# Block-2 modulation vectors: four matmuls against a column of ones in place of four transposes and a row sum

## The reference, cut to what matters

```python
cond = jax.nn.silu(c)                       # (1, 1024)
for l in range(DEPTH):
    mod = cond @ ada_w[l] + ada_b[l]        # ada_w[l]: 1024 x 9216
    sh1, sc1, ga1, sh2, sc2, ga2, sh3, sc3, ga3 = jnp.split(mod, 9, axis=-1)
    n = _modulate(_rms_norm(h, norm_g[l, 0]), sh1, sc1)
    h = h + 0.5 * ga1 * _swiglu(n, ffn_w_in[l, 0], ffn_w_out[l, 0])
    ...
```

## Time and profile before

| | before |
|---|---|
| median of 3 runs | 2551.77 us (2551.61 to 2553.09) |
| profiled execution, its own time | 2551.77 us |
| its span (first to last instruction) | 2550.0 us |
| mean granted TensorE clock | 0.986 of full speed |
| busy share: TensorE matmul / weight load | 96% / 82% |
| busy share: VectorE / ScalarE / GpSimd | 65% / 47% / 8% |

### The profile page before, as it was taken

The page is one execution under the profiler, slowest core; times in us unless marked ns, Lnnn a source line. Parts: engine busy times, 40 slices in busy tenths (PEclk is TensorE's granted clock), DMA queues, the critical chain, the costliest instruction groups (busy, mean ns, idle before and its releaser), DMA issues.

```text
span 2550.0 us, 34014 instructions
## 1 busy us (share of the span) xinstructions
PE 2447.2 (96%) x13945; PEld 2086.7 (82%) x13945; DVE 1656.3 (65%) x2149; ACT 1202.5 (47%) x1441; POOL 215.2 (8%) x334
## 2 busy tenths in 40 slices
PE   7999999999999999899999999989999999998998
PEld 5888998788788899788788798878877879887886
DVE  4786777787776686778668665575555456557444
ACT  4445464444443546443444436944444443694443
POOL 2000002000100000300010000210000000021000
PEclk9999999999999999999999999999999999999999
DMA  8784455786887454688588554455556545445553
GB/s 291 260 298 149 148 166 190 256 297 231 274 292 235 132 158 156 221 272 297 179 275 304 184 158 133 133 180 188 200 168 206 189 152 157 136 131 184 198 182 103
DMA packets 369162, 514.25 MB, mean 202 GB/s; under 512 B 21600, under 2 KB 310614, under 8 KB 369008
## 3 DMA queue, kind: packets, MB, share of 16 engines
q1 hardware_dynamic: 342608, 415.80, 50.6%
q0 software_dynamic: 26400, 96.28, 10.7%
HBM read 510.89 MB, written 1.13 MB: 201 GB/s over the span
## 4 chain that ended last, share of the span: by engine, by line
PE 83%; DVE 8%; ACT 4%; issue 3%; POOL 1%; DMA 0%; SPq 0%; DVEq 0%; POOLq 0%; ACTq 0%
PE ps L1658 76%; DVE lo L1083 3%; ACT hi L708 2%; PE ps L1704 2%; PE ps L1680 1%; PE ps L1834 1%; PE ps L1844 1%; DVE arena L1572 1%; POOL T L641 1%; PE ps L1806 1%; DVE arena L1142 1%; PE ps L1853 1%; ACT arena L748 0%; DMA raw<-in_ffn_w_gu 0%; DVE X L1116 0%
## 5 line engine op out<-in xcount | busy, mean ns | idle before, releaser
L1083 DVE TENSOR_TENSOR lo<-raw,hi 128x2048 fp32r<-128x2048 f32 (+1 forms) x400 | 908.5, 2273 | 541.8 <-ACT hi L708 541.0
L708 ACT ACTIVATE hi<-raw 128x2048 fp32r<-128x2048 f32 (+1 forms) x400 | 757.7, 1897 | 508.4 <-PE ps L1658 494.4
L1658 PE MATMUL ps<-hi,NH 128*128 128x512 f32 (+3 forms) x1760 | 681.5, 387 | 38.1 <-DVE lo L1083 14.8
L1658 PE MATMUL ps<-hi,NL 128*128 128x512 f32 (+3 forms) x1760 | 672.3, 382 | 0.0
L1658 PE MATMUL ps<-lo,NH 128*128 128x512 f32 (+3 forms) x1760 | 671.9, 382 | 0.0
L1658 PEld LDWEIGHTS ps<-hi,NH 128*128 128x128 f32 x1760 | 337.2, 192 | 114.2 <-DVE lo L1083 32.1
L1658 PE MATMUL ps<-NH,hi 128*128 128x256 f32 x1376 | 394.9, 287 | 0.0
L1658 PEld LDWEIGHTS ps<-hi,NL 128*128 128x128 f32 x1760 | 336.3, 191 | 66.5
L1658 PEld LDWEIGHTS ps<-lo,NH 128*128 128x128 f32 x1760 | 337.2, 192 | 64.1
L1658 PE MATMUL ps<-NL,hi 128*128 128x256 f32 x1376 | 388.7, 282 | 0.0
L1658 PE MATMUL ps<-NH,lo 128*128 128x256 f32 x1376 | 387.4, 282 | 0.0
(11 more groups left out here) (297 smaller groups left out, 2025.8 us busy)
## 6 DMA issues: line engine op xcount, KB each, us to landing
raw<-in_ffn_w_gu SPq DMA_DIRECT2D x176, 512.0 KB, 5.1
raw<-in_ffn_w_in SPq DMA_DIRECT2D x176, 512.0 KB, 4.8
arena<-in_ada_w POOLq DMA_DIRECT2D x72, 1024.0 KB, 7.4
raw<-in_w_in SPq DMA_DIRECT2D x96, 512.0 KB, 4.5
raw<-in_ffn_w_down SPq DMA_DIRECT2D x88, 512.0 KB, 4.7
raw<-in_ffn_w_out SPq DMA_DIRECT2D x88, 512.0 KB, 4.1
raw<-in_mix_w_in SPq DMA_DIRECT2D x86, 512.0 KB, 4.6
raw<-in_w_branch SPq DMA_DIRECT2D x16, 512.0 KB, 4.0
```

The costliest lines, as they stand in the source:

```text
L708: last = nc.scalar.activation(dst, src, ACT.Copy)
L1083: last = nc.vector.tensor_tensor(dst, src, part.bitcast(F32), ALU.subtract)
L1658: last = nc.tensor.matmul(dst, a, b, start=start and k == 0, stop=stop and k == 2, skip_group_check=skip)
```

## The change

The four transposes of a chunk become four matmuls: each 128 x 128 piece of `ada_acc` is the stationary operand (as it was in the transpose), and the moving operand is one column of ones instead of the 128-column identity. The result of each is the sum over partitions, one column of PSUM. The row sum on VectorE becomes a copy of four columns.

```diff
@@ ada_keep (VectorE) @@
                 dve.wait_ge(pe_done, at("pe", f"ada {a}"))
-                nc.vector.tensor_reduce(mods[:, 4 * a:4 * a + 4], ps[:, 2, :].rearrange("p (k n) -> p k n", k=4), AX.X, ALU.add).then_inc(dve_done, done("dve", f"mods {a}"))
+                nc.vector.tensor_copy(mods[:, 4 * a:4 * a + 4], ps[:, 2, 0:4]).then_inc(dve_done, done("dve", f"mods {a}"))
@@ extras (TensorE) @@
                     pe.wait_ge(dve_done, at("dve", f"ada {a} 7"))
                     for k in range(4):
-                        last = nc.tensor.transpose(ps[:, 2, P * k:P * k + P], ada_acc[:, P * k:P * k + P], ident)
+                        last = nc.tensor.matmul(ps[:, 2, k:k + 1], ada_acc[:, P * k:P * k + P], tri[:, P:P + 1], start=True, stop=True)
                     last.then_inc(pe_done, done("pe", f"ada {a}"))
```

## The result

The changed kernel takes 2571.05 us (median of 4 runs, 2569.10 to 2572.24), the kernel before 2551.69 us (4 runs, 2549.41 to 2553.09). The ratio is 1.0076, with a 95% interval of 1.0058 to 1.0094: slower by 0.76%. The change does what it says, both on TensorE and on VectorE, and loses.

What follows compares the result with a forecast made beforehand. TensorE's instruction queue was taken to bound the edited bodies, with VectorE's saving worth nothing; 36 x (0.88 - 0.44) = +15.8 us on 2551.8 gave 2567.6 us, 0.6% slower, range 2562 to 2572.

Steps and rivals of the forecast that it cites:

- The bound: In the 36 edited feed-forward bodies, TensorE's instruction queue sets the time: 122.00 of 122.00 us busy, VectorE 94.88.
- The moving columns: In the four matmuls of a chunk, streaming 1 column instead of 128 saves about nothing.
- Two records per call: On the edited line, a plain fp32 matmul is two records, each with its own weight load: eight per chunk, not four.
- The load sets the spacing: In the edited chunks, each record is spaced by its 128-column weight load, about 0.111 us.
- column-spaced rival: Small matmuls in the chunk follow each other by columns, 0.03 us each: 7.2 us saved, 2544.6 us; chance 0.05.
- The price of 0.22 per call: Each of the chunk's four matmuls costs 0.22 us, 0.88 in place of 0.44 for the transposes.
- three places: Few-column calls priced elsewhere in the kernel: L2034 0.22 us, L2021 and L2022 0.43 at half clock, L2043 0.18.
- the remaining cover of 0.6: In an edited body, VectorE's copy still comes 0.6 us after TensorE's longer chunk ends, so VectorE won't wait.
- +0.44 us for each chunk: On TensorE in each of 36 bodies, the matmuls' added cost over the transposes, 0.88 against 0.44; +15.8 us in all.
- More than doubled: Edited chunks cost 0.89 against 0.39 us: +18 us, 2569.8; within the forecast range, no chance of its own.
- The signs: Changed profile: 288 records about 0.11 us apart, 0.88 booked for eight, body 17.9 us, DVE down 17 to 22, PE waits unchanged.
- The VectorE rival: Splits in edited bodies end earlier and free a waiting TensorE, returning up to 18 us: 2549.6 us; chance 0.01.

Runs made afterwards that it cites:

- e4_no_partition_sum: Kernel before without the four transposes and their waits, mods filled with a constant, sum over partitions left out: 2534.51 us against 2550.98, ratio 0.9938.
- e1_copy_only: Kernel before with only the VectorE half of the change, the 128x512 reduction becoming a 128x4 copy, transposes kept: 2550.74 us against 2550.98, ratio 1.0001.
- e2_identity_matmul: Kernel before with each transpose written as a plain fp32 matmul against the 128-column identity, reduction kept: 2568.6 us against 2550.98, ratio 1.0072.
- e5_after_again: The changed kernel unaltered, timed again on a second chip against the kernel before: 2568.73 us against 2550.78, ratio 1.0068.

## Why the prediction was right

*The bound.* TensorE's queue bounds the edited bodies, before and after: the chain there is TensorE alone in both traces, and taking its work out gave 16.5 us back (e4_no_partition_sum). Shown.

*The moving columns.* I held that they are worth nothing. 1 column (2568.73, ratio 1.0068) and 128 columns (2568.6, ratio 1.0072) take the same time. Shown.

*Two records per call.* 288 records on the line; with 144 of the same width the time is back at 2552.78, and 576 cost 28.5 us more than 288. Shown.

*The load sets the spacing.* 0.111 us per record with a load of 128 columns, in the sixteen-record version too, and 0.025 with a load of one column. Shown for plain fp32, for these two widths. The column-spaced rival is out: its 0.03 us per record is what records take when the loads are narrow, which is not this change.

*The price of 0.22 per call.* It came out right, but in part by luck. The first of its three places, L2034 and L2035, doesn't show what I read from it. L2035 loads 16 columns and not 128, so its 0.22 us isn't the price of two wide loads. And the step from L2034's second record to L2035, 0.19 us, holds a load that was not started early, as its own row shows:

```profile
1582.01 0.30 PEld L2034 LDWEIGHTS ps<-arena 128*128 128x128 f32 x2
1582.34 0.11 PEld L2035 LDWEIGHTS ps<-arena 128*16 128x16 f32 x2
```

The first load of L2034 begins 0.11 us ahead of its matmul (1582.12), that of L2035 with its matmul (1582.34). What carries the forecast is the long stream of the earlier trace rows, 0.111 us a step with 128-column loads throughout. The records of the changed kernel keep the same step.

*VectorE.* The copy took 155 ns, I had 0.2 us. Busy time fell by 19.1 us, in the 17 to 22 forecast, and was worth 0.2 us alone (e1_copy_only), within the scatter. The copy came 0.69 us after the last record (129.98 against 128.34 + 0.95), as the remaining cover of 0.6 said.

*The size.* I forecast 2567.6 us, that is +15.8; measured are +19.4 on the first chip and +18.0 on the second, inside the range of 2562 to 2572, on the first chip within 1 us of its upper end. The term that was too small is "+0.44 us for each chunk". By the starts of matmuls it is 0.46: from the last ordinary matmul before the chunk to the second one after it, 1.36 us (128.11 to 129.47) against 0.90 (127.46 to 128.36):

```profile
127.46 0.39 PE L1658 MATMUL ps<-hi,NL 128*128 128x512 f32 x1
128.36 0.40 PE L1658 MATMUL ps<-lo,NH 128*128 128x512 f32 x1
```

The body of the earlier trace rows grew by 0.52, the average body by 0.50. The other 0.06 of that body is spread over the ordinary matmuls; part of it shows as 5.57 us for a stretch of 24 that took 5.54 before. The kernel before has such stretches of 5.57 too, in its third edited stage, and the body with four fp32r records is 0.05 over 17.49 as well. So it doesn't come with the second records, but what makes it was not found. I had kept the whole-body price of the transposes (0.39) for the range and used 0.44 in the sum. With 17.10 and 17.49 from the bodies and 8 x 0.111 on the other side it would have come to +18 us, closer to what was measured. That sum stands in the prediction as the rival "More than doubled", 2569.8; the two measured gains fit it better than my own case.

*The signs.* 288 records, 0.111 us apart after the first, VectorE's 19.1 us and no new wait of TensorE are as forecast, the body is 18.01 us and not 17.9. The chain books 0.79 us for the eight, not 0.88, although their starts are spaced as expected. It goes from end to end, and a record with one column ends sooner than one with 128: the same eight records with 128 columns are booked 0.89 (e2_identity_matmul).

*A slip in the rivals.* The VectorE rival was priced at 2549.6, which is 2.2 us under the kernel before. By the prediction's own limit of 5 us that is no change, and not "faster".

*The clock.* It is 0.986 on average in both, 1.00 in the edited bodies. Low-clock stretches of the mixing stages move with the work. In the profiled run after, the last one is longer than before, as the busy table of that stretch shows (PEclk is the third number from the end), 10.1 us at 0.50; the same work before went at 0.67:

```profile
2208.40:2218.50 10.10, 7.38 (x24) 6.52 (x25) 4.87 (x6) 0.97 (x1) 2.52 (x5) 0.50 0.34 104
```
```profile
2192.40:2202.50 10.10, 7.48 (x44) 6.91 (x45) 4.77 (x6) 1.42 (x3) 2.42 (x5) 0.67 0.34 104
```

That is 10.1 x (0.67 - 0.50) = 1.7 us of full-clock work, the size that I had allowed one stretch. It is scatter and not a price of the change, as the changed kernel itself has that stretch short on the second chip (e5_after_again):

```profile
2209.30:2219.50 10.20, 7.47 (x44) 6.91 (x45) 4.88 (x7) 1.53 (x3) 2.52 (x5) 0.67 0.34 104
```

## What to carry to other kernels

Count a small matmul by its records and by the width of what it loads, not by what it streams: here a plain fp32 matmul was two loads of 128 columns, a transpose one, and moving 128 columns cost no more than moving one. Where TensorE has no wait in a stretch, a saving on another engine is worth nothing there (19 us of VectorE's time gave 0.2 us), and the same saving read the other way is room: a sum over partitions that VectorE did in 1.4 us of idle time beat both TensorE forms. Where in that engine's order the work goes decides whether the room is real, as 0.1 us a body was lost and regained by moving two instructions.

## What the runs showed of the hardware that I had not expected

A weight load is not always started beside the matmul ahead of it. In the run with loads of one column the first such load of a chunk began only with its own matmul: PEld idled 0.37 us before it, 13.1 us over 36 chunks. The body came out 0.10 us longer than with four transposes, although the records themselves take 0.025 us each. But narrow loads as such can start early: within the chunk each load starts 0.02 us ahead of its matmul. What was late were the loads at which the number of loaded columns changes, at 127.81 from 128 columns to one and at 128.08 back to 128. The kernel before shows the same from 128 to 16 columns between L2034 and L2035 (1582.34).

It isn't a rule without exception. In the kernel before, a load of 72 columns behind loads of 128 did start 0.11 us ahead of its matmul:

```profile
1171.24 0.11 PEld L1816 LDWEIGHTS ps<-arena 128*72 128x72 f32 x1
1171.35 0.27 PE L1816 MATMUL ps<-arena 128*72 128x128 f32 x1
```

That one is a transpose, the others are plain matmuls. No run separates the kind of instruction from the width, so which of them decides stays open.
